# One-hot groups between first products of more tiles ahead, their activations spilled to DRAM

## The reference, cut to what matters

```
q  = h @ w_query                          # 8 heads, 2 halves of 128
sc = q . sub_keys                         # 128 scores for each half
v1, i1 = top_k(sc[0], 16); v2, i2 = top_k(sc[1], 16)
top_s, pos = top_k(v1[:, None] + v2[None, :], 16)
idx = take(i1 * 128 + i2, pos); g = softmax(top_s)     # 8 x 16 = 128 picks per token
act = gelu(h . expert_u[idx]);  out = sum(g * act * expert_v[idx])
```

## Time and profile before

| | |
|---|---|
| median of 3 runs | 1521.38 us (1519.65 to 1522.84) |
| profiled execution, its own time | 1520.39 us |
| its span | 1518.2 us |
| PE busy | 1477.2 us, 97% of the span |
| PEld busy | 1297.6 us, 85% |
| DVE busy | 908.6 us, 60% |
| ACT busy | 848.6 us, 56% |
| POOL busy | 548.8 us, 36% |
| HBM read, written | 236.21 MB, 1.05 MB |
| granted PE clock | 0.997 of full speed |

### The profile page before, as it was taken

One profiled execution on the slowest core, in us unless ns is written; L12 is line 12 of the kernel. 1 busy time (PEld: TensorE's weight loads), 2 busy tenths in 40 slices (PEclk: granted clock), 3 DMA queues, 4 the chain that ended last, 5 costly groups with the idle time before them and its releaser, 6 DMA issues.

```text
span 1518.2 us, 24600 instructions
## 1 busy us (share of the span) xinstructions
PE 1477.2 (97%) x8779; PEld 1297.6 (85%) x8779; DVE 908.6 (60%) x2191; ACT 848.6 (56%) x1597; POOL 548.8 (36%) x214
## 2 busy tenths in 40 slices
PE   7999999999999999989999999999999999999998
PEld 6788888788899898889999888888888888888786
DVE  4935259388245531225996976666666666666665
ACT  5556454588356644443557975555555555555554
POOL 6881665700567477455888940000000000000000
PEclk9999999999999999999999999999999999999999
DMA  8750445600334344332551035555555555555564
GB/s 316 280 173 29 166 135 173 220 29 2 111 137 159 122 161 173 139 118 105 181 180 57 1 139 191 187 186 187 191 192 193 193 193 187 187 186 190 179 194 136
DMA packets 43699, 238.36 MB, mean 157 GB/s; under 512 B 4320, under 2 KB 4448, under 8 KB 25440
## 3 DMA queue, kind: packets, MB, share of 16 engines
q1 hardware_dynamic: 43616, 237.27, 45.5%
HBM read 236.21 MB, written 1.05 MB: 156 GB/s over the span
## 4 chain that ended last, share of the span: by engine, by line
PE 64%; ACT 3%; POOL 2%; DVE 2%; issue 1%; ACTq 0%; DVEq 0%
PE bank L1254 23%; PE bank L1277 11%; PE bank L840 6%; PE bank L1280 6%; PE bank L673 4%; PE bank L793 2%; POOL wlo L1321 2%; PE bank L1234 2%; PE bank L676 2%; PE bank L735 1%; PE bank L776 1%; ACT whi L1393 1%; ACT arena L1707 1%; PE bank L969 1%; PE bank L1121 1%
## 5 line engine op out<-in xcount | busy, mean ns | idle before, releaser
L1321 POOL TENSOR_TENSOR wlo<-raw,whi 128x2048 fp32r<-128x2048 f32 (+1 forms) x51 | 195.2, 3839 | 159.2 <-ACT whi L1393 158.9
L1321 POOL TENSOR_TENSOR wlo<-arena,whi 128x2048 fp32r<-128x2048 f32 (+1 forms) x45 | 195.0, 4339 | 152.7 <-ACT whi L1393 152.6
L1254 PE MATMUL bank<-whi,ghi 128*128 128x512 f32 x512 | 200.7, 392 | 1.7 <-DVE glo L2500 1.0
L1254 PE MATMUL bank<-wlo,ghi 128*128 128x512 f32 x512 | 200.4, 391 | 0.0
L1254 PE MATMUL bank<-whi,glo 128*128 128x512 f32 x512 | 199.2, 389 | 0.0
L1277 PE MATMUL bank<-hT,whi 128*128 128x512 f32 x768 | 189.9, 389 | 1.6 <-ACT whi L1739 1.6
L1277 PEld LDWEIGHTS bank<-hT,whi 128*128 128x128 f32 x768 | 144.0, 188 | 31.7 <-ACT whi L1739 1.8
L2487 DVE TENSOR_TENSOR wlo<-raw,whi 128x1024 fp32r<-128x1024 f32 x84 | 102.8, 1225 | 70.6 <-ACT whi L1746 70.6
L1393 ACT ACTIVATE whi<-arena 128x2048 fp32r<-128x2048 f32 x41 | 78.4, 1915 | 95.1 <-PE bank L793 28.7
L1746 ACT ACTIVATE whi<-raw 128x1024 fp32r<-128x1024 f32 x84 | 88.7, 1057 | 76.3 <-PE bank L1254 73.8
L793 PE MATMUL bank<-whi,hT 128*128 128x512 f32 x512 | 125.8, 392 | 0.0
(11 more groups left out here) (333 smaller groups left out, 3047.9 us busy)
## 6 DMA issues: line engine op xcount, KB each, us to landing
raw<-ex_in SPq DMA_DIRECT2D x64, 1024.0 KB, 4.8
raw<-w_in SPq DMA_DIRECT2D x44, 1024.0 KB, 5.2
arena<-w_in SPq DMA_DIRECT2D x44, 1024.0 KB, 5.2
xw<-ex_in SPq DMA_DIRECT2D x32, 1024.0 KB, 4.8
raw<-ex_in SPq DMA_DIRECT2D x54, 512.0 KB, 4.2
xw<-ex_in SPq DMA_DIRECT2D x10, 512.0 KB, 4.3
arena<-frt_in SPq DMA_DIRECT2D x1, 3904.0 KB, 15.6
arena<-tab_in SPq DMA_DIRECT2D x1, 1089.0 KB, 18.6
```

Source lines behind the costliest of these rows:

```text
L1254: last = mm(bank[2 * t + h][:, :], g[:, j % 2, tok], w[:, b, at], start=False, stop=(final and i == 2), skip_group_check=True)
L1321: last = G.tensor_tensor(wlo[:, u % 2, at], slots[u % RING][:, at], whi[:, u % 2, at], ALU.subtract)
```

## The change

The loop gets 80 tiles instead of 98, and 48 instead of 30 are ahead. From tile 29 of these on, each of 16 tiles is followed by two groups on PE (`groups_at`), so that the 32 groups stand between first products. One quarter slot and its two split slots become buffers of the one-hots, which have two buffers instead of four; the ring of slots for u is three from tile 24 on (RAW_OF, SPLIT_OF). Groups use two banks (6 and 7), and the products of tiles 29 to 45 bank 5. "sel1" is transposed after tile 27 instead of 28. The products of tiles 0 and 1 come after tile 47.

`arena` now holds gate weights of all 128 tiles, so that there is no room for the activations. ACT writes them to three small places in turn (`staged`), SP stores them to a tensor in DRAM (`spill`, 128 KB a tile, 1 KB per partition). In the tail SP loads each back into the part of `arena` of tiles that are done, and DVE multiplies it with the weights (`weigh_again`); POOL's weighing is gone. ACT copies each bank in one instruction of 512 elements, in token order (runs of 4 in `arena`, PSUM read with a stride of 512 B). ACT gates one of 8 tokens and POOL 7. The loops of `w_groups` are written out.

```diff
-NL = 2 + XBODY * 16
+NL = 2 + XBODY * 13
-ACT_GATES = 2
+ACT_GATES = 1
 SEL0_AT = 19
-SEL1_AT = 28
+SEL1_AT = 27
+G0 = 29
+GROUPS_W = T // 8
+G1 = G0 + GROUPS_W // 2
+HEAD = [(NA + 2 * tile + part, tile, part) for tile in range(2) for part in range(2)]
+RAW_OF = [i % 4 if i < G0 - 5 else i % 3 for i in range(NA)] + [0, 1, 2, 0]
+SPLIT_OF = [i % 4 if i < G0 - 5 else i % 3 for i in range(NA)] + [0, 1, 2, 3]
+LAST_OF_FOUR = G0 - 6
+def groups_at(i):
+    return range(2 * (i - G0), 2 * (i - G0) + 2) if G0 <= i < G1 else range(0)
...
+        first_hot = [w.rearrange("p (j n) -> p j n", j=8) for w in (aslots[3], xw[:, D:2 * D])]
+        second_hot = [w.rearrange("p (j n) -> p j n", j=8) for w in (ahi[3], alo[3])]
+        staged = [gact[:, 0], gact[:, 1], xw[:, 3 * T:4 * T]]
+        spill = nc.dram_tensor("spill", (NA, P, T), FP32, kind="Internal").ap()
...
         @block.sync
+            def store_act(i):
+                sp_.wait_ge(aa_gelu, i + 1)
+                sp_.dma_start(spill[i], staged[i % 3]).then_inc(act_stored[i % 3], 16)
+            for i in range(NA + 4):
...
+                    sp_.wait_ge(aulo_ready, before(RAW_OF, i) + 1)
...
+                sp_.dma_start(aslots[RAW_OF[i]], rows_of_u).then_inc(aex_loaded[RAW_OF[i]], 16)
+                if i >= 6:
+                    store_act(i - 6)
...
             for i in range(2, 2 + XRING):
+                sp_.wait_ge(aulo_ready, NA + 3 if i == 2 else NA + 4)
+                sp_.wait_ge(wt_done, T // 4)
+                for k in range(3):
+                    sp_.wait_ge(act_stored[k], 16 * (NA // 3))
                 sp_.dma_start(xslots[ex_slot(i)], ex_d[i]).then_inc(ex_loaded[ex_slot(i)], 16)
...
             for i in range(NL, N_KEYS):
                 sp_.wait_ge(vlo_ready, i - XRING - 1)
                 sp_.dma_start(xslots[ex_slot(i)][:, D:2 * D], ex_d[i][:, D:2 * D]).then_inc(ex_loaded[ex_slot(i)], 16)
+                m = i - NL
+                if m >= 4:
+                    sp_.wait_ge(g_ready, i - 3)
+                sp_.dma_start(act_again[m], spill[m]).then_inc(act_back[m % 4], 16)
...
         @block.tensor
+            def w_group(n):
+                first, second = first_hot[n % 2], second_hot[n % 2].bitcast(FP32)
+                pe.wait_ge(hotB, n + 1)
+                pe.wait_ge(hotA, n + 1)
+                pe.wait_ge(hotC, n + 1)
+                for h in range(2):
+                    if n == 0:
+                        pe.wait_ge(aa_gelu, G0 - h)
+                    else:
+                        pe.wait_ge(wt_taken, 8 + 2 * (n - 1) + h + 1)
+                    for j in range(4):
+                        last = mm(wbank[h][:, P * j:P * j + P], first[:, 4 * h + j, :], second[:, 4 * h + j, :],
+                                  start=True, stop=True)
+                    last.then_inc(wt_done, 1)
             for i in range(NA):
...
+                early_product(i, aa_done)
                 if i == SEL0_AT:
                     transposes("sel0")
                 if i == SEL1_AT:
                     transposes("sel1")
+                for n in groups_at(i):
+                    w_group(n)
...
         @block.gpsimd
+            for i in range(NA + 4):
                 pool.wait_ge(auhi_ready, i + 1)
+                G.tensor_tensor(alo[SPLIT_OF[i]], aslots[RAW_OF[i]], ahi[SPLIT_OF[i]], ALU.subtract).then_inc(aulo_ready, 1)
+                for n in groups_at(i - 1):
+                    w_gates(n)
...
         @block.scalar
+            W4 = arena[:, :].rearrange("p (n g t) -> p g t n", g=T // 4, t=4)
+            def w_out(n):
+                for h in range(2):
+                    act.wait_ge(wt_done, 2 * n + h + 1)
+                    A(W4[:, 2 * n + h].rearrange("p t n -> p n t"), wbank[h][:, :].rearrange("p (t n) -> p n t", t=4),
+                      ACT.Copy).then_inc(wt_taken, 1)
...
             for i in range(NA):
                 act.wait_ge(aa_done, i + 1)
+                if i >= 3:
+                    act.wait_ge(act_stored[i % 3], 16 * (i // 3))
+                A(staged[i % 3], early_bank(i)[:, 0:T], ACT.Gelu_apprx_tanh).then_inc(aa_gelu, 1)
+                for n in groups_at(i):
+                    w_out(n)
+                for j in range(i + 1, NA + 3):
+                    if before(SPLIT_OF, j) == i:
+                        ahead_hi(j)
+                for n in groups_at(i + 1):
+                    w_gates(n)
...
+            act.wait_ge(wt_done, T // 4)
+            act.wait_ge(aex_loaded[RAW_OF[NA + 3]], 16 * RAW_OF.count(RAW_OF[NA + 3]))
+            A(ahi[SPLIT_OF[NA + 3]], aslots[RAW_OF[NA + 3]], ACT.Copy).then_inc(auhi_ready, 1)
+            for n in range(2):
+                head_gelu(n)
...
         @block.vector
+            def w_group(n):
+                if n == 0:
+                    dve.wait_ge(aulo_ready, LAST_OF_FOUR + 1)
+                if n >= 2:
+                    dve.wait_ge(wt_done, 2 * n - 2)
...
+            def weigh_again(i):
...
+                    dve.wait_ge(act_back[m % 4], 16 * (m // 4 + 1))
+                    V.tensor_tensor(w, act_again[m], w, ALU.mult).then_inc(g_ready, 1)
...
             for i in range(NL, N_KEYS):
                 dve.wait_ge(ghi_ready, i + 1)
+                V.tensor_tensor(glo[:, i % 2, :], Wg[:, T * i:T * i + T], ghi[:, i % 2, :], ALU.subtract).then_inc(glo_ready, 1)
+                weigh_again(i + 1)
                 tail_lo(i + 2)
```

More of the change, by code:

```diff
@@ L31, with before @@
 XBODY = 6
-NL = 2 + XBODY * 16
+NL = 2 + XBODY * 13
 NA = N_KEYS - NL
 E_AT = (12, 23)
-ACT_GATES = 2
+ACT_GATES = 1
 SEL0_AT = 19
-SEL1_AT = 28
+SEL1_AT = 27
[6 more added lines that the diff above has]
+LAST_OF_FOUR = G0 - 6
+def before(ring, i):
+    earlier = [j for j in range(i) if ring[j] == ring[i]]
+    return earlier[-1] if earlier else None
+def groups_at(i):
+    return range(2 * (i - G0), 2 * (i - G0) + 2) if G0 <= i < G1 else range(0)
 SCALE = HD ** -0.5
@@ L392, in build @@
         iota_ps = bank[4][:, 0:P]
-        wbank = bank[5:8]
-        kept_w = [xw[:, 3 * T + 8 * NA * i:3 * T + 8 * NA * i + 8 * NA].rearrange("p (n t) -> p n t", t=8) for i in range(3)]
+        wbank = bank[6:8]
         QP = R[:, 0:4096].rearrange("p (b t) -> p b t", b=16)
@@ L519, in build, with early_bank @@
         ysq = arena[:, 3 * D:3 * D + CW]
[L521 to L525, removed]
+        head_bank = [bank[5 + (NA + n - G1) % 3] for n in range(2)]
+        head_first = [q for q in HEAD if q[2] == 0]
+        def early_bank(i):
+            return bank[6 + i % 2] if i < G0 else bank[5] if i <= G1 else bank[5 + (i - G1) % 3]
         def ex_slot(i):
@@ L1687, in ahead_hi, with w_gates @@
                 else:
-                    act.wait_ge(aa_done, i - 3)
-                A(ahi[i % 4], aslots[i % 4], ACT.Copy).then_inc(auhi_ready, 1)
+                    act.wait_ge(aa_done, before(SPLIT_OF, i) + 1)
+                A(ahi[SPLIT_OF[i]], aslots[RAW_OF[i]], ACT.Copy).then_inc(auhi_ready, 1)
+            W4 = arena[:, :].rearrange("p (n g t) -> p g t n", g=T // 4, t=4)
[4 more added lines that the diff above has]
+                      ACT.Copy).then_inc(wt_taken, 1)
+            def w_gates(n):
+                hot = first_hot[n % 2]
+                act.wait_ge(hot_ready, n + 1)
+                for j in range(8 - ACT_GATES, 8):
+                    last = A(hot[:, j, :], hot[:, j, :], ACT.Copy, scale=gates[:, n, j:j + 1])
+                last.then_inc(hotC, 1)
             for i in range(4):
@@ L1694, in _ @@
                 act.wait_ge(aa_done, i + 1)
-                A(ahead_act[i], bank[6 + i % 2][:, 0:T], ACT.Gelu_apprx_tanh).then_inc(aa_gelu, 1)
-                ahead_hi(i + 4)
+                if i >= 3:
[8 more added lines that the diff above has]
+                    w_gates(n)
                 if i in E_AT:
@@ L1715, in head_gelu @@
                 act.wait_ge(a_done, n + 1)
[L1716 to L1735 removed]
+                act.wait_ge(act_stored[n], 16 * (NA // 3))
+                A(gact[:, tile, :], head_bank[n][:, 0:T], ACT.Gelu_apprx_tanh).then_inc(a_gelu, 1)
+            act.wait_ge(wt_done, T // 4)
[3 more added lines that the diff above has]
+                head_gelu(n)
             def hi_u(i):
```

154 lines of the change are left out of this document (47 added, 107 removed).

## The result

The changed kernel takes 1509.96 us (median of 4 runs, 1508.14 to 1510.13) against 1520.77 for the kernel before on the same chip (4 runs, 1519.65 to 1522.84): a ratio of 0.9925, 95% interval 0.9907 to 0.9942. The profiled execution took 1509.89 us, with a span of 1508.1. By these medians the gain is 10.8 us, where 7.4 were forecast; when both kernels were measured on another chip it was 7.4 (1519.38 for the kernel before in 13 runs, 1511.94 for the changed one in 4).

The account below looks back on a forecast made before the run. PE, 97% busy, bounds the kernel, losing some 0.4 us in each of 32 groups. Stretch terms sum to 214.9 against 222.3: gain 7.4, so 1513.0, plus 1.0 for the median, 1514.0 us; wider range 1509.5 to 1521.5.

Parts of the forecast that it names:

- The start of the groups: Where groups begin among the tiles ahead: PE loses 0.5 us (0 to 1.0) to fewer slots, queued stores and POOL's work.
- the waits in the mixed tiles: In the 16 tiles each followed by two groups: PE waits 0.1 us each, 1.6 in all (0 to 0.4 each).
- the hole: Before tiles 0 and 1's second products: PE idles for GELU and DVE's weighing, rounding and remainder, 2.8 us (2.1 to 3.4).
- the second products behind the hole: Second products of tiles 0 and 1 on PE: 5.55 us, unchanged from the kernel before.
- the 1.62 us ahead of tile 4: PE's idle time before loop tile 4: goes, because three megabytes of loads arrive before tile 4 is wanted.
- its own bounds: Whole kernel's time: 1511.2 to 1516.8 us, from low and high values of waits, hole and start, and the 1.62 kept.
- A group at 1.85 us: Group stage on PE: an unheld group takes 1.85 us, read at the last query scores; 32 groups take 59.2.
- the rival built on it: Groups beside fp32r products: each costs PE its present busy time, 2.13 us; +9, about 1523 us; chance 0.08.
- The copy at 0.60 us: ACT's token-order copy of 512 elements from a group's bank: 0.60 us, in time for PE; high end 1.10.
- transposes and fill: PE's transposes and the fill at either end of the tiles ahead: 1.2 us, unchanged.
- Tail 2.72 us a tile, transfer hidden: Tail of 48 tiles: PE keeps 2.72 us each; reloading spilled tiles costs zero, at most 2.3 us of DMA per tile.
- POOL sets the pace: Rival in the mixed tiles: gates cost what remainders do, POOL needs 6.6 us per tile; +4.8, near 1518.8; chance 0.09.

Follow-up runs that it names:

- all helpers relieved: Kernel before, with second one-hots built for 2 tokens of 8, ACT's gates cut to 8 elements, POOL's to 3 tokens; result incomplete; 1508.35 us.
- the filler: Changed kernel plus eight unread matmuls of 512 columns into an unused bank behind tile 1's first product; 1510.2 us, ratio 0.9933.
- the heads moved: Changed kernel with the first products of tiles 0 and 1 placed before tiles 46 and 47; 1508.25 us, ratio 0.9921.
- tile 4 first: Tile 4's u rounded before ACT's and DVE's remaining tile 2 work: 1508.44 us with tiles 0 and 1's first products moved earlier, 1511.99 on the changed kernel alone.
- DVE relieved: Kernel before, with the second one-hot of each group from group 4 on built for 2 tokens of 8 only; result incomplete; 1519.87 us.

## Why the prediction had the mechanism right and the number wrong

The mechanism held: 32 groups no longer wait for DVE and ACT, because between two pairs of them PE makes a first product. The steps that failed are these.

- The idle time in the sum was too large. The start of the groups (0.5), the waits in the mixed tiles (1.6) and the hole (2.8) made 4.9 us; measured were 0, 0 and 1.88.
- Two costs were put at nothing: the second products behind the hole were called unchanged at 5.55 us and took 7.20, and the 1.62 us ahead of tile 4 was to go and stayed.
- The step from the gain to the time took one profiled execution as fixed. It subtracted 7.4 from it and added 1.0 for the median, and its own bounds left no room for what moves without any change.

The first two cancel nearly, and it is luck that the 7.4 us of gain came out so near the 7.6 measured in the stretch. The third holds most of the distance to 1509.96. Term by term:

- *A group at 1.85 us*. Right. The 16 mixed tiles last 105.0 us; less 16 x 2.88 that is 58.9 for the groups, against 59.2. The run with all helpers relieved gives 59.77 for 32 groups by another way. The busy time of 68.05 us was stretched by the waits, and the rival built on it (2.13 us a group) fell.
- *The copy at 0.60 us.* Right, and it was the step that decided most: the other order costs 7.45 us in the mixed part. The choice of the row nearest in its order of writing, not in its size, was the right one.
- *Start of the groups 0.5, waits 16 x 0.1.* Both wrong, both 0. The working above them had found over 1 us of room for each wait, and the sum then booked a price all the same. With the groups' 0.3 and 0.15 less for transposes and fill, this is 2.55 us of gain that was not forecast.
- *The hole at 2.8 us.* It was 1.88, below the low end of 2.1: POOL's last remainder ended just before DVE's multiplications began, so that these were quick. 0.9 us of gain not forecast.
- *Behind the hole 5.55 us, "unchanged".* Wrong by 1.65 us of loss. It was taken from a place where PE came in at full clock. After 1.88 us of idle time the clock fell to half for 3.4 us of the second products. No price for it stood in the sum or in the rivals. That it hangs on the hole is shown by the filler (5.59) and by the heads moved (5.46); that not every such hole brings it is shown by the copy in tile order (5.61 behind a longer hole).
- *The 1.62 us ahead of tile 4 goes.* Wrong by 1.62 us. The prediction looked at when the loads land, and not at what ACT has to do between the products of tiles 2 and 4: the copy, v, GELU and rounding, in an order that the change leaves alone. It was 1.62 in every run that leaves tiles 0, 1 and 4 in their order, and 1.54 with the heads moved alone; where ACT's order was changed it went, but only without the heads moved, and most of the time was lost again at tile 5.
- *Tail 2.72 us a tile, transfer hidden.* Right. 565.25 us from tile 2's product to the last matmul, where 615.06 less 18 x 2.76 gives 565.38.
- *POOL sets the pace.* It fell: a gate product took 1.68 us (1.72 said), a remainder 2.36, and POOL waited for the one-hots 12.6 us.

In sum for the stretch: 214.85 said, 213.03 measured (-2.55 - 0.9 + 1.65); for the same work before, 222.3 said, of which 1.62 was no gain. So 7.4 said and 7.6 measured, by errors of +1.62 and -1.8 that cancel. The rest of the distance to 1509.96 is not shown to be of the change. The span fell by 10.1: 7.60 in the stretch, 1.67 because the stretch began at 723.70 and not at 725.37, 0.13 in the loop and tail, 0.69 behind the last matmul (6.82 and 6.13; the kernel before again has 6.2). The device time was 2.2 us above the span before and 1.8 after, which is another 0.4, and the 1.0 that was added for the median did not come back. With the 0.2 of the stretch that is, to 0.1 us, the 4.0 us by which the forecast was too high. The repeated runs show that start and end move by as much with no change at all; all runs of the changed kernel reach from 1508.14 to 1513.71. Why the stretch starts 4 us later in some runs is only partly seen: between 660 and 672 us, where both kernels have the same instructions, the granted clock was 0.72 in the kernel before and 0.86 in the changed one of the first pair. The rows, of before and of after:

```profile
660.00:672.00 12.00, 8.48 (x51) 8.44 (x52) 6.15 (x17) 5.53 (x12) 4.55 (x1) 0.72 0.47 165
```

```profile
660.00:672.00 12.00, 9.38 (x61) 8.73 (x62) 7.47 (x20) 4.63 (x10) 4.56 (x1) 0.86 0.46 171
```

Of all thirteen profiles the four with 0.86 start the stretch at 723.6 to 723.9, the nine with 0.72 at 724.4 to 728.1. What sets that was not tried, so the cause of this part stays open.

The version with the heads' first products two tiles earlier is the fastest that was run. Its medians, 1508.25 and 1508.44 (with tile 4 first), overlap the changed kernel's 1509.96 and 1511.94 in their single runs; the 3.6 us in the stretch are what can be told apart.

## What to carry to other kernels

Where several helpers look full at once, relieving one gives little; put other work of the bound engine between, so that all of them get room, and price the stage at what that engine takes alone, read at a place where nobody holds it. When a transfer is said to be hidden or a wait to go, follow the helper's whole list of instructions up to it, not only the transfer, and see who waits next once the wait is gone. A hole in PE's work is to be priced with what follows it, since the clock behind it may be half.

## What the runs showed of the hardware

- After 1.9 us of idle time PE's granted clock went down to half for some 3.4 us (matmuls of 512 columns every 0.42 us instead of 0.23). It did so in four of the five runs with such a hole; in the run with the copy in tile order, with a hole of 2.04 us, it did not. That run had also let PE wait 0.34 us in each mixed tile before; whether that is the reason was not tried. The 1.62 us ahead of tile 4 never did it. So a hole near 2 us costs up to 1.65 us more than itself.
- A copy by ACT of 512 elements from PSUM takes 0.60 us when it reads with a stride of 512 bytes and writes runs of 16 bytes, and 1.08 us when it reads without a stride and writes one element in each KB.
- Two DVE multiplications of 128 elements with both inputs in SBUF took 0.49 us alone, 1.76 and 2.41 us beside POOL.
- ACT's lengths in a profile are not prices: with DVE relieved the same copy of 392 elements is recorded at 1220 ns and not 843, at a pace that is a little quicker (2.21 and not 2.24 us a group). The line of the group stage of that run:

```profile
L1707 ACT ACTIVATE arena<-bank 128x392 f32 x46 | 46.6, 1220 | 0.0
```
